# Gated value outputs in passes of 512 columns, the dense second product in two other banks, and two orders around the attention pairs of a two-block fp32 transformer kernel

## What is computed

```python
def squared_relu_mlp(h, w1, w2):                       # dense MLP, D_FF = 4096
    return jnp.square(jax.nn.relu(h @ w1)) @ w2
...
for layer in range(DEPTH):                             # second block, DEPTH = 2
    ...
    x = x + moba_out.reshape(B, S, N_MOBA_HEADS * HEAD_DIM) @ w_out_odd[i]
    x = x + conv_glu_ffn(rmsnorm(x, ffn_norm[layer]), w_up[layer], conv_w[layer], conv_b[layer], w_down[layer])
```

## Time and profile before

| | |
|---|---|
| median of 3 runs | 1144.67 us (1144.58 to 2714.05) |
| profiled execution | 1145.06 us, its span (first to last instruction) 1143.1 us |
| mean granted TensorE clock | 0.999 of full |
| busy: TensorE, VectorE, ScalarE, GpSimd | 1128.9, 867.6, 668.0, 127.5 us |
| HBM | 206.59 MB moved, 180 GB/s over the span |

### The profile page before, as it was taken

One profiled execution on the slowest core, in us unless ns is written; L12 is line 12 of the kernel. 1 busy time (PEld: TensorE's weight loads), 2 busy tenths in 40 slices (PEclk: granted clock), 3 DMA queues, 4 the chain that ended last, 5 costly groups with the idle time before them and its releaser, 6 DMA issues.

```text
span 1143.1 us, 24264 instructions
## 1 busy us (share of the span) xinstructions
PE 1128.9 (99%) x9301; PEld 850.7 (74%) x9301; DVE 867.6 (76%) x1435; ACT 668.0 (58%) x1074; POOL 127.5 (11%) x168
## 2 busy tenths in 40 slices
PE   8999999999999999999999999999999999999998
PEld 6768866666888866666877788887667678888865
DVE  7787988866777988755769869876776666978685
ACT  7665677534567577533575767564455666755432
POOL 0000200000203200000242310000124431000010
PEclk9999999999999999999999999999999999999999
DMA  8762365565563366565352447654664344765451
GB/s 345 264 204 75 124 227 202 180 218 191 175 230 107 115 231 211 185 219 199 134 188 108 152 144 232 211 166 147 200 254 154 124 146 157 240 201 180 153 175 64
DMA packets 31468, 206.59 MB, mean 181 GB/s; under 512 B 3488, under 2 KB 3872, under 8 KB 10144
## 3 DMA queue, kind: packets, MB, share of 16 engines
q1 hardware_dynamic: 31104, 205.00, 52.3%
q10 hardware_dynamic: 288, 0.52, 0.1%
HBM read 204.46 MB, written 1.05 MB: 180 GB/s over the span
## 4 chain that ended last, share of the span: by engine, by line
PE 92%; DVE 4%; ACT 2%; DMA 1%; issue 1%; POOL 0%; SPq 0%; DVEq 0%
PE ps L653 14%; PE ps L642 10%; PE ps L643 10%; PE ps L644 10%; PE ps L654 7%; PE ps L1093 7%; PE ps L1094 4%; PE ps L1007 1%; PE ps L1543 1%; PE ps L1287 1%; PE ps L915 1%; PE ps L1544 1%; PE ps L1545 1%; PE ps L1288 1%; PE ps L1289 1%; PE ps L916 1%
## 5 line engine op out<-in xcount | busy, mean ns | idle before, releaser
L1631 ACT ACTIVATE w_hi<-staged 128x2048 f16<-128x2048 f32 (+3 forms) x191 | 337.8, 1785 | 193.2 <-PE ps L654 133.0
L2428 DVE SCALAR_TENSOR_TENSOR w_lo<-staged,w_hi 128x2048 f16<-128x2048 f32 (+3 forms) x191 | 408.6, 2152 | 17.0 <-ACT w_hi L1631 15.9
L653 PE MATMUL ps<-both,w_hi 128*128 128x512 f16 x756 | 245.9, 379 | 0.0
L643 PE MATMUL ps<-both,w_hi 128*128 128x256 f16 x768 | 209.3, 273 | 0.0
L642 PE MATMUL ps<-both,w_hi 128*128 128x256 f16 x768 | 209.3, 273 | 0.0
L644 PE MATMUL ps<-both,w_lo 128*128 128x256 f16 x768 | 209.3, 273 | 0.0
L654 PE MATMUL ps<-both,w_lo 128*128 128x256 f16 x756 | 206.1, 273 | 0.0
L653 PEld LDWEIGHTS ps<-both,w_hi 128*128 128x128 f16 x756 | 74.0, 98 | 88.7
L1093 PE MATMUL ps<-x_both,w_hi 128*128 128x512 f16 x384 | 124.9, 379 | 0.0
L1094 PE MATMUL ps<-x_both,w_lo 128*128 128x256 f16 x384 | 104.7, 273 | 0.0
L643 PEld LDWEIGHTS ps<-both,w_hi 128*128 128x128 f16 x768 | 75.1, 98 | 9.5
(11 more groups left out here) (410 smaller groups left out, 2129.2 us busy)
## 6 DMA issues: line engine op xcount, KB each, us to landing
staged<-weights SPq DMA_DIRECT2D x165, 1024.0 KB, 5.2
staged<-weights SPq DMA_DIRECT2D x32, 704.0 KB, 4.3
xn<-bands SPq DMA_DIRECT2D x3, 512.0 KB, 10.2
m<-bands SPq DMA_DIRECT2D x3, 512.0 KB, 8.3
cst<-constants SPq DMA_DIRECT2D x1, 1027.0 KB, 7.9
h<-x_turned SPq DMA_DIRECT2D x2, 512.0 KB, 4.8
staged<-weights SPq DMA_DIRECT2D x2, 512.0 KB, 7.3
qT<-bands SPq DMA_DIRECT2D x2, 512.0 KB, 11.5
```

Source lines behind the costliest of these rows:

```text
L643: pe.matmul(out, wh, xl[:, c, :], start=False, stop=False)
L653: pe.matmul(out, wh, both[:, :, c, :], start=(c == 0), stop=False)
L1631: act.activation(w_hi[:, s, o:o + n], staged[:, s, o:o + n], ACT.Copy, scale=SW).then_inc(hi_split, 1)
L2428: dve.scalar_tensor_tensor(w_lo[:, s, o:o + n], staged[:, s, o:o + n], SW, w_hi[:, s, o:o + n], ALU.mult, ALU.subtract).then_inc(lo_split, 1)
```

## The change

Five edits.

1. In the up stages of both gated MLPs each value output but the first of a layer is made the wide way. ScalarE copies the second half of the bank into `scores` after the product and ahead of its weight half; in the next turn VectorE adds the first half to it, and the multiplication with the gate reads the sum.
2. The second product of the dense MLPs lies in banks 4 and 5 instead of 0 and 1. The wait for two more drained banks of the first product goes.
3. In the even layer the second `latent_values` goes from ahead of score pair 4 to behind the transposes of pair 3.
4. In the odd layer ScalarE takes raw row (1, 1) out ahead of the exponentials of pair 0 instead of behind them.
5. In the odd layer the swap of pair 1 stands, as for the other pairs, after the first four chunks of the next product and not after all eight.

```diff
--- before.py
+++ after.py
@@ -71,6 +71,8 @@
 TAKEN = -3e38
 
 RING = 4
+
+DENSE_BANK = 4
 
 
 TURN_LAG, OUT_LAG, UP_LAG = 3, 4, 2
@@ -1101,7 +1103,6 @@
                     for n in range(8):
                         hidden_chunk(i, n)
 
-                pe.wait_ge(drained[one], FC - RING + 2)
                 pe.sem_inc(drained[two], 2)
                 u0 = FIRST[two]
 
@@ -1109,14 +1110,14 @@
 
                     pe.wait_ge(lo_split, i * 4 + (2 * (u0 + s) + 2))
                     pe.wait_ge(drained[two], i * 2 + (s + 1))
-                    wide(ps[:, s, :], (u0 + s) % 2, FC, fresh).then_inc(product[two], 1)
+                    wide(ps[:, DENSE_BANK + s, :], (u0 + s) % 2, FC, fresh).then_inc(product[two], 1)
 
                 def last_output(c):
 
                     wh, wl = weights((u0 + 1) % 2, P * c, P)
-                    pe.matmul(ps[:, 1, 0:T], wh, f_hi[:, c, :], start=(c == 0), stop=False)
-                    pe.matmul(ps[:, 1, 0:T], wh, f_lo[:, c, :], start=False, stop=False)
-                    return pe.matmul(ps[:, 1, 0:T], wl, f_hi[:, c, :], start=False, stop=(c == FC - 1))
+                    pe.matmul(ps[:, DENSE_BANK + 1, 0:T], wh, f_hi[:, c, :], start=(c == 0), stop=False)
+                    pe.matmul(ps[:, DENSE_BANK + 1, 0:T], wh, f_lo[:, c, :], start=False, stop=False)
+                    return pe.matmul(ps[:, DENSE_BANK + 1, 0:T], wl, f_hi[:, c, :], start=False, stop=(c == FC - 1))
 
                 last = dict(STREAM)[two] // 2 - 1
                 with pe.Fori(0, last) as i:
@@ -1408,9 +1409,9 @@
             swap_query(0)
             chunk(16, 5, D, DC // 2, DC)
             latent_values(0)
-            latent_values(1)
             score_pair("even", 4)
             turn_pair("even", 3)
+            latent_values(1)
             latent_keys(1)
             out_pair("even", 3)
 
@@ -1477,7 +1478,11 @@
                         wait_from(pe, drained[up], i * 4 + (n - 1))
                         features(ps[:, j, 0:T], sl, 2 * j * DC * P, DC, *g_in).then_inc(product[up], 1)
                         wait_from(pe, u_drained[layer], i * 4 + (n - 3))
-                        features(ps[:, 2 + n, 0:T], sl, (2 * j + 1) * DC * P, DC, *g_in).then_inc(u_product[layer], 1)
+                        for c in range(DC):
+                            wh, wl = weights(sl, ((2 * j + 1) * DC + c) * P, P)
+                            pe.matmul(ps[:, 2 + n, :], wh, both[:, :, FC - DC + c, :], start=(c == 0), stop=False)
+                            last = pe.matmul(ps[:, 2 + n, 0:T], wl, g_in[0][:, c, :], start=False, stop=(c == DC - 1))
+                        last.then_inc(u_product[layer], 1)
 
 
                 pe.wait_ge(h_ready[("oute", "outo")[layer]], DC - 1)
@@ -1566,11 +1571,8 @@
             last_pair = MOBA_HEADS // 2 - 1
             for p in range(last_pair):
                 pair_product(p + 1, 0, 0, DC // 2)
-                if p != 1:
-                    swap_pair(p)
+                swap_pair(p)
                 pair_product(p + 1, 0, DC // 2, DC)
-                if p == 1:
-                    swap_pair(p)
                 pair_product(p + 1, 1, 0, DC // 2)
                 score_pair("moba", p)
                 if p:
@@ -1958,7 +1960,7 @@
                 else:
                     unit(units // 2 - 1, 0)
                     last_halves(two, 0)
-                last_square(product[two], units + 1, ps[:, 1, 0:T], INVF)
+                last_square(product[two], units + 1, ps[:, DENSE_BANK + 1, 0:T], INVF)
                 root(f"ffn_post_{layer}")
 
             def last_halves(name, e):
@@ -2186,6 +2188,9 @@
                     if new:
 
                         act.wait_ge(u_product[layer], i * 4 + (n + 1))
+                        if n or not isinstance(i, int):
+                            wait_from(act, u_drained[layer], i * 4 + (n - 1))
+                            act.activation(scores[:, n % 2, 0:T], ps[:, 2 + n % 4, T:2 * T], ACT.Copy).then_inc(second_copied, 1)
                         hi(g, g // 2 % 2, i * 16 + 16 * (g // 4 + 1), size, o + size * (g % 2))
 
                         act.wait_ge(g_conv[layer], i * 8 + (2 * n + 2))
@@ -2254,15 +2259,16 @@
             ODD_SPLITS = ((4, 5), (4, 6), (6, 7), (8, 8), (10, 9), (16, 12), (18, 13, 14))
             for p in range(last_pair):
                 if p != VALUES_AFTER + 1:
-                    raw(p, 1)
+                    if p != 1:
+                        raw(p, 1)
                     if p >= 2:
                         high_pair("moba", p - 2)
                 split_after(*ODD_SPLITS[p])
                 raw(p + 1, 0)
                 if p:
                     turned_pair("moba", p - 1)
-                if p == last_pair - 1:
-                    raw(last_pair, 1)
+                if p in (0, last_pair - 1):
+                    raw(p + 1, 1)
                 exp_pair("moba", p)
                 if p == VALUES_AFTER:
                     raw(p + 1, 1)
@@ -2840,11 +2846,11 @@
                         dve.wait_ge(last_squared, BY_TOKEN.index(f"ffn_post_{layer}") + 1)
                     mc = m[:, bass.ds(i * 2 + s, 1), :]
                     if ended:
-                        dve.tensor_scalar(mc, ps[:, s:s + 1, 0:T], INVF, None, ALU.mult).then_inc(drained[two], 1)
+                        dve.tensor_scalar(mc, ps[:, DENSE_BANK + s:DENSE_BANK + s + 1, 0:T], INVF, None, ALU.mult).then_inc(drained[two], 1)
                     else:
-                        dve.tensor_scalar(mc, ps[:, s:s + 1, 0:T], INVF, None, ALU.mult).then_inc(high_taken, 1)
+                        dve.tensor_scalar(mc, ps[:, DENSE_BANK + s:DENSE_BANK + s + 1, 0:T], INVF, None, ALU.mult).then_inc(high_taken, 1)
                         dve.wait_ge(high_taken, i * 2 + (layer * (DC - 1) + s + 1))
-                        dve.scalar_tensor_tensor(mc, ps[:, s:s + 1, T:2 * T], INVF, mc, ALU.mult, ALU.add).then_inc(drained[two], 1)
+                        dve.scalar_tensor_tensor(mc, ps[:, DENSE_BANK + s:DENSE_BANK + s + 1, T:2 * T], INVF, mc, ALU.mult, ALU.add).then_inc(drained[two], 1)
                     if splits or squares:
                         dve.wait_ge(drained[two], i * 2 + (s + 3))
                         add_square(mc, s, ADDED_AT[f"ffn_post_{layer}"] + s, (i, 2))
@@ -3076,8 +3082,15 @@
                     if old:
 
                         dve.wait_ge(u_product[layer], i * 4 + n)
+                        src = ps[:, 2 + (n - 1) % 4, 0:T]
+                        if n > 1 or not isinstance(i, int):
+                            made = i * 4 + (2 * (FC - 8) + layer * (GC - 1) + n - 1)
+                            src = scores[:, 1 - j, 0:T]
+                            dve.wait_ge(second_copied, made)
+                            dve.tensor_tensor(src, ps[:, 2 + (n - 1) % 4, 0:T], src, ALU.add).then_inc(parts_added, 1)
+                            dve.wait_ge(parts_added, made)
                         dve.wait_ge(g_silu[layer], i * 4 + n)
-                        dve.scalar_tensor_tensor(tmp[:, 3 - j, :], ps[:, 2 + (n - 1) % 4, 0:T], INV, tmp[:, 1 - j, :],
+                        dve.scalar_tensor_tensor(tmp[:, 3 - j, :], src, INV, tmp[:, 1 - j, :],
                                                  ALU.mult, ALU.mult).then_inc(u_drained[layer], 1)
                         o, size = halves
                         lo(g // 2 % 2, g % 2, i * 4 + (g + 1), size, o + size * (g % 2))
```

## The result

| | before | after |
|---|---|---|
| median | 1144.68 us (18 runs, 1144.32 to 1145.16, but for one of 2714.05) | 1147.23 us (18 runs, 1145.23 to 1148.14) |
| ratio | | 1.0019, 95% interval 1.0013 to 1.0026 |
| profiled execution, its span | 1145.06, 1143.1 us | 1147.83, 1145.5 us |
| granted TensorE clock, mean | 0.999 | 0.998 |

What follows compares the result with a forecast made beforehand. TensorE was taken as the bound, busy 1128.9 of 1143.1 us. Terms -0.7 + 0 + 0 - 0.1 + 0.5 = -0.3 gave 1144.8 us on the profiled execution, 1144.4 on the median; range 1142.6 to 1146.2.

Steps and rivals of the forecast that it cites:

- The pace of the wide pass: Up stages: 336 steps of the value outputs, each 2.2 ns shorter with the 512-column pass, -0.7 us.
- its copies and adds cost nothing: Up stages: the 84 new ScalarE and VectorE instructions hide in VectorE's 0.92 us of waiting per turn; 0.46 us stay.
- The dense banks: Second dense product in banks 4 and 5: the removed wait was already over, so 0 us.
- The even layer: Latent value 1 behind the transposes: transposes start at 631.83, query swap at 636.8 instead of 636.86, -0.1 us.
- the head of the chain: Odd layer: exposed table load makes the first exponential 2.15 us later, and VectorE's low half 0.55 us later.
- The scores of pair 1: Odd layer: they start at 875.97 for 875.78, +0.2 us, waiting for the exponentials instead of their swap.
- GpSimd's division and cosine row shift with the exponentials and stay beside it: Odd layer: low half keeps nearly its 2.82 us beside GpSimd, so key swap 2 comes late, +0.5 us.
- a sign that I had named as wrong: Odd layer: key swap 2 without a wait was listed among the signs that would show the forecast wrong.
- The orders do their work: Rival, even and odd layers: the load is hidden and three idle times of 1.30 us go, -2.0 us, 1142.7; chance 0.20.
- The dearer load: Rival, odd layer: the exposed table load costs up to 1.4 us more than its row shows, 1145.8 us; chance 0.12.
- VectorE the bound of the up loops: Rival, up stages: each turn grows 0.36 us too much for VectorE, +14 us, 1158 us; chance 0.03.
- no saving by the wide form: Rival, up stages: the 512-column pass saves nothing here, +0.4 us in all, 1145.1 us; chance 0.07.

Runs made afterwards that it cites:

- preload_low_late: Changed kernel plus a one-element exponential ahead of raw row (1,1), and VectorE's low half of weight half 6 behind the maxima of pair 1: 1143.27 us.
- raw_only: Kernel before with only raw row (1,1) moved ahead of the exponentials of pair 0, key swap 1 left in place: 1148.30 us.
- odd_only: Kernel before with only the two odd-layer orders, the earlier raw row (1,1) and the earlier key swap 1: 1148.29 us.
- after_preload: Changed kernel plus a one-element exponential ahead of raw row (1,1), so ScalarE loads its table while waiting: 1144.51 us.

## Why the prediction was wrong, step by step

**Right.** The pace of the wide pass: -0.7 predicted, -0.84 in the trace (2 x 0.42), -0.65 by the medians. That its copies and adds cost nothing: VectorE's turn in the up loop after, which answers to the earlier trace rows,

```profile
724.36 0.42 DVE L3080 TENSOR_TENSOR pad<-ps,stat 128x256 f32<-128x256 f32 x1 [0.44 <-PE ps L646]
...
729.58 0.43 DVE L3080 TENSOR_TENSOR pad<-ps,stat 128x256 f32<-128x256 f32 x1 [0.43 <-PE ps L646]
```

has 0.44 us of waiting left of 0.92, and repeats every 5.22 us for 5.24. The dense banks: 0, and the products 0.10 us apart at the boundary. The even layer: the transposes at 631.67, with the offset of 0.15 at 631.82, for 631.83 predicted; the swap at 636.77 for 636.8. The second is in part luck. I had TensorE come to it last, at 636.8; it came at 636.5 (its last matmul before starts at 636.21 and lasts 0.27) or 636.6 with the offset, and then waited, by the times for VectorE's step of the keys,

```profile
635.77 0.75 DVE L2951 TENSOR_TENSOR kT<-ps,m 128x256 f32<-128x256 f32 x2
```

over at 636.52, 0.10 us ahead of the swap as in before. TensorE was early because the moved product added 0.75 us between the start of the transposes and that of the next chunk (3.33 for 2.58), where I had 0.91.

In the odd layer the head of the chain was right too: the first exponential comes at 871.87, and taking back the 0.66 that TensorE was ahead there it is 2.18 us later than before, for 2.15; the low half is 0.57 later, for 0.55.

**A term of the sum mis-sized.** The scores of pair 1 came 0.47 later for 0.2. The second step of the rotation, L3179, took 0.99 us where I had left its length of before, 0.69 (L3166, below): the later reciprocal released GpSimd's division directly ahead of it, and it began while an operation of the division ran.

**The step that failed.** "GpSimd's division and cosine row shift with the exponentials and stay beside it." I read the low half's 2.82 us (for 2.28) as a price that VectorE pays for GpSimd's company, and priced only VectorE. The rows show an exclusion in both directions, in which the one that comes second pays. The rows of before that I should have read it from, VectorE and GpSimd:

```profile
875.04 0.69 DVE L3166 TENSOR_TENSOR qT<-qT,tmp 128x512 f32<-128x512 f32 x1
...
875.10 1.22 POOL L2392 TENSOR_TENSOR qT<-kT,tmp 128x256 f32<-128x256 f32 x1
```

The cosine row L2392 (0.73 us when alone) began within L3166 and paid 0.5 us; it ran until 876.32, and the low half, which began at 875.65, paid 0.54. Before, the division was over at 875.14: it and the low half never met. Shifting the division by 2.15 - 0.66 and the low half by 0.57 - 0.66 laid one across the other. GpSimd's last operation found VectorE at work and stood for two microseconds, and TensorE's transposes, behind the scores, wait for exactly that division. The prediction never followed that wait in the odd layer, though it had named it in the even one. This was worth 1.95 us, and drew the clock's 1.6 behind it, for which the sum had no term at all. +0.5 became +3.5. The other half of that step failed too: with the cosine row behind the division (at 878.38) instead of beside it, the low half took 2.38 us, not 2.82. And a sign that I had named as wrong came, key swap 2 without a wait, though not because its raw row was early: TensorE came there 2.94 us later than before.

The Trainium skill (SBUF — State Buffer, Who interferes with whom) states this rule: VectorE and GpSimd share a pair of ports under an exclusive lock, a VectorE instruction with two SBUF inputs contends with a GpSimd instruction that reads SBUF, and the one that issues second "fully blocks". The runs agree with the rule as far as they show it: the division takes 1.90 us when it meets no such operation, 2.35 with the rotation's second step, 4.40 with that and the low half, and its last part ends behind the low half; and the rotation's first step L3176, with one of its two inputs in PSUM, took 0.66 us beside the division, not longer than before. That ports are the reason, no run here shows. A look at that page could have turned the 2.82 us from a stretch into an order of arrival.

**The rivals.** *The orders do their work* did not come about here, but in preload_low_late it did: -1.7 us against before, where I had priced it at -2.0. *The dearer load* (1145.8) had the time nearest to the measured one, still 1.4 us short, but its reason didn't hold: the exponential started 871.87 - 870.57 = 1.30 us after the load began, with no drain behind it. The second figure of the Trainium skill (ScalarE: Activation LUTs, What ACT_TABLE_LOAD costs), 1380 ns of drain, shows neither here nor at the load at 685.42. *VectorE the bound of the up loops* (1158) and *no saving by the wide form* fell by the rows above. The range failed because its upper end for the odd layer (+0.7) came from rows of VectorE alone.

## What to carry to other kernels

When a change shifts one of two engines that share something, don't move their old durations along: list for both, in order of time, which operations each will meet afterwards, and who waits for the one that is blocked. A long filler (here the half-weight conversion of VectorE, which nobody waits for) can be put where the partner has nothing urgent; that alone was worth 3.6 us here. And an operation that is moved ahead of a table load can push the load out of idle time and into the chain (here by 2.18 us); a tiny operation that needs the coming table, put where the engine idles anyway, hid it again (-0.65 us, from 1143.92 to 1143.27).

## What I had not expected of the hardware

- A small operation of GpSimd can take over four times its length behind one long VectorE operation: 2.65 us for 0.61, read in one row. The group's mean hides it; the narrow window shows it.
- TensorE's clock fell from 2.4 to 1.2 GHz behind waits of 0.66 and 1.95 us and stayed there for some 3.4 us, but not in each run: of the profiled executions with these waits two show the fall (the changed kernel, raw_only) and one doesn't (odd_only). The gap between the clusters of the changed kernel, whose medians are 1147.36 and 1145.76, fits the 1.6 us that the fall costs in the trace. The mean granted clock of each run speaks for it: 0.9974 on average in the 13 runs of the upper cluster, 0.9992 in the 5 of the lower, where half the clock for 3.4 of 1145 us is 0.0015. Run by run it is not shown: the clock of a run is given to 0.001, and 2 of the 5 lie at 0.998. after_preload, with one wait of 1.25 us, has neither the fall nor a second cluster.
